# A hybrid layer's projection in another order, with modulation slabs inside it and its blocks gathered by GpSimd

## The chip, the cores and the metric

The kernel runs on one core of one Trainium2 chip, in one launch. The metric is the device time of that launch in microseconds (us), lower is better. Engines are named as the profile names them: PE is TensorE (PEld its weight loads), DVE is VectorE, ACT is ScalarE, POOL is GpSimd, SP is SyncE, which here only issues DMAs.

## The reference

The program is a chain of small layers over 256 tokens of width 1024, all in float32: a hybrid mixer, a conformer convolution, two HGRN mixers, an mLSTM, an S5 mixer, each with a feed-forward layer behind it. Only the first, the hybrid mixer, is touched. Of it:

```python
def ada_terms(cond, w_mod, b_mod):
    m = jax.nn.silu(cond) @ w_mod + b_mod          # "modulation": 6 x 1024 values a layer
    return jnp.split(m, 6, axis=-1)

def split_hybrid_projection(p, conv_w, a_log, dt_bias, q_norm, k_norm):
    qkv = jax.nn.silu(depthwise_conv_centred(p[..., :OFF_Z_A], conv_w))
    ...
    qa = l2_normalize(qkv[:, :, 0]) * (A_HEAD_DIM ** -0.5)
    ka = l2_normalize(qkv[:, :, 1])
    va = qkv[:, :, 2]
    za = p[..., OFF_Z_A:OFF_BA_A]
    beta = jax.nn.sigmoid(ba[:, :, 0])
    g = -jnp.exp(a_log) * jax.nn.softplus(ba[:, :, 1] + dt_bias)
    qb = rms_norm(p[..., OFF_Q_B:OFF_K_B], q_norm)
    kb = rms_norm(p[..., OFF_K_B:OFF_V_B], k_norm)
    vb = p[..., OFF_V_B:]

def gated_delta_chunked(q, k, v, g, beta, s0, need_out):
    ...
    lower = jnp.where(strict, jnp.einsum("nbhcd,nbhsd->nbhcs", kb, kc) * decay, 0.0)
    sol = lax.linalg.triangular_solve(lower + eye, rhs, left_side=True, lower=True, unit_diagonal=True)
```

The mixer projects 256 latent and 256 context tokens, runs a gated delta rule in both directions over four heads ("A"), an attention with eight query heads over two key heads ("B"), and multiplies both results, side by side, by `w_out`. The kernel works the triangular solves out as inverses of 128 x 128 unit lower triangular matrices, 32 of them.

## The kernel before

**Stages.** Each engine has its own program, the stages' parts in order; nothing reorders them. Here the stages are `Front`, `HybridProjection`, `BlockInverse` (which only has work on POOL under its own name), `HybridAttention`, `Delta`, `DeltaReadout`, `BackgroundEnd`, `OutProjection`. Engines meet at semaphores (`wait_ge`, `then_inc`). PE's results go to seven PSUM banks in rotation (`k.job`): a job waits until the bank's user before it is done. An eighth bank belongs to the modulation.

**Weights** come as slabs of 128 x 2048 floats (1 MB) from one DRAM array in the order of use, into a ring of five (`RING`); SP issues the load of a slab once PE is done with the slab five places earlier.

**Projection.** 22 chunks `n` of 128 output features, two to a slab, each eight accumulating matmuls (line 216) over 512 tokens, or 256 where only the latent tokens are wanted. Order: keys A (n 0 to 3, 512 wide), queries A (4 to 7, 256), queries B (8 to 11, 256), keys B and values B (12, 13), values A (14 to 17, 512), the gate z (18 to 21, 256). After n = 8 PE computes the delta rule's gates (line 1331). ACT takes each chunk out of PSUM (lines 1373, 1377); for keys, queries and values A DVE applies a convolution of five taps (lines 1462, 1464), and ACT a silu (1341). The head norms of 13 heads (`heads`): ACT squares (1349), PE sums by a matmul with ones (1305, placed by `sums_after`), ACT takes Ln and Exp (1357, 1360), DVE multiplies (1477). Between the chunks lie also the products of the lower triangles (`lower_after`, lines 1742, 1749, 1729, and on DVE 1808 to 1824) and five rope products (1319), which DVE uses in `rotate` (1488 to 1492).

**Blocks.** The inverses start with their 32 x 32 diagonal blocks, 4 per matrix: `early` (DVE) brings them into one layout by four transposes of 32 partitions each (line 1869), then forward substitution runs in 31 steps of two DVE instructions (`step`, lines 1892 and 1893), ten of them at once and two in each unit of the attention; after units 12 and 13 `scatter_turned` and `scatter` write them back by four transposes each (1899, 1906). `Delta` needs them.

**Attention.** 16 units u. PE: scores (1542), a modulation slab, then for the unit before, four transposes of the probabilities (1550), and every second unit the product with the values (1560), in the others one more modulation slab. ACT: Exp (1577), the copies (470, 1588). DVE: maximum and scaling (1599 to 1604), block steps, copy of the output (1612).

**Background modulation.** `w_mod` has 48 slabs; eight are used in `Front`, 40 lie behind the projection's eleven in the array. `fill(pe, 2)` runs one slab: two small matmuls that turn the row of the slab before (line 398, which wait for ACT's copy at line 470), and eight with the slab (216, `weight_ring,silu_cond`). 25 slabs run in the attention, 8 in `Delta`, and the rest in `BackgroundEnd`, in front of the output projection:

```python
def finish(self, pe):
    self.fill(pe, 2 * len(self.work))
    self.turn(pe, len(self.work) - 1).then_inc(self.done[0], 1)
```

`DeltaReadout` normalizes the delta rule's output in two halves t: ACT copy and square (2259, 2261), PE sum (2252), ACT Ln (2266) and Exp (2269), DVE (2278 to 2283).

## Time and profile before

| | us |
|---|---|
| median of 3 runs | 2736.01 |
| lowest and highest of them | 2727.53, 2738.37 |
| profiled execution | 2733.76 |
| its span in the trace | 2731.9 |

| engine | busy us | share of the span |
|---|---|---|
| PE | 2425.6 | 89% |
| PEld | 2169.8 | 79% |
| DVE | 1556.2 | 57% |
| ACT | 1064.9 | 39% |
| POOL | 90.0 | 3% |

Busy time counts instructions that do work; PE's ends are modelled, so a busy PE isn't PE at its peak. PE has a granted clock, given by the profile as a share of full speed: 1.00 is 2.4 GHz and 0.50 is 1.2 GHz. Of the chain of work that ended last PE holds 79%, DVE 13%, ACT 5%. The hybrid mixer takes the first 460 us or so of the span.

### The profile page before, as it was taken

To read this page: it belongs to the slowest core of one execution; us is meant where nothing else is said; L and a number is where in the kernel's file an instruction comes from. 1 tells how busy PE (TensorE), PEld (TensorE's weight loads), DVE (VectorE), ACT (ScalarE), POOL (GpSimd) and SP (SyncE) were. 2 spreads that over 40 slices of the span, in tenths; PEclk is the share of its full clock that TensorE was granted. 3 is DMA by queue.
4 is the path that set the end of the run, shared out by engine and by line. 5 is a ranking of instruction groups with operands and counts; after the bars stand their busy time and mean duration, and the time that the engine had idled before them with its cause. 6 is when DMAs were issued, how large, how long until landed. Compare 5 with 4: busy or idle time off the path is not lost.

```text
span 2731.9 us, 40134 instructions
## 1 busy us (share of the span) xinstructions
PE 2425.6 (89%) x16978; PEld 2169.8 (79%) x16978; DVE 1556.2 (57%) x2585; ACT 1064.9 (39%) x1675; POOL 90.0 (3%) x107
## 2 busy tenths in 40 slices
PE   7989888999979999768998978998998999748998
PEld 3655666998868998758997858997678998746998
DVE  3475542654846544565657446556955556664655
ACT  2433232434334445333434424434524435623443
POOL 0010000000000000000000000003600000000000
PEclk8998897999999999888999869999999999978999
DMA  7216334553224554203553304552024554301552
GB/s 288 92 63 258 113 125 168 201 186 139 93 77 170 185 185 140 93 1 145 190 190 108 124 17 168 185 184 96 1 77 159 184 185 152 138 1 47 198 189 78
DMA packets 50291, 368.25 MB, mean 135 GB/s; under 512 B 5568, under 2 KB 5696, under 8 KB 5824
## 3 DMA queue, kind: packets, MB, share of 16 engines
q1 hardware_dynamic: 49968, 363.59, 36.6%
q8 instruction: 134, 2.20, 0.3%
q10 hardware_dynamic: 144, 2.10, 0.2%
q14 instruction: 45, 0.37, 0.0%
HBM read 364.62 MB, written 1.05 MB: 134 GB/s over the span
## 4 chain that ended last, share of the span: by engine, by line
PE 79%; DVE 13%; ACT 5%; issue 2%; DMA 1%; SPq 0%; DVEq 0%; ACTq 0%
PE psum L216 63%; PE psum L2755 3%; DVE weight_parts L209 1%; PE psum L3344 1%; PE psum L3345 1%; PE psum L398 1%; PE psum L2378 1%; PE psum L3081 1%; DVE work L947 1%; DMA weight_ring<-stream_dram 1%; PE psum L1560 1%; DVE work L2829 1%; DVE work L2830 1%; PE psum L3362 1%; PE psum L543 1%
## 5 line engine op out<-in xcount | busy, mean ns | idle before, releaser
L216 PE MATMUL psum<-input_parts,weight_parts 128*128 128x256 f32 x7872 | 959.6, 285 | 52.8 <-DVE input_parts L955 27.3
L216 PEld LDWEIGHTS psum<-input_parts,weight_parts 128*128 128x128 f32 x7872 | 954.4, 192 | 60.5 <-issue 54.4
L209 DVE TENSOR_TENSOR weight_parts<-weight_ring,weight_parts 128x1024 fp32r<-128x1024 f32 x484 | 570.5, 1220 | 319.0 <-ACT weight_parts L193 318.4
L193 ACT ACTIVATE weight_parts<-weight_ring 128x1024 fp32r<-128x1024 f32 x484 | 485.3, 1053 | 199.0 <-PE psum L216 193.4
L216 PE MATMUL psum<-work,weight_ring 128*128 128x256 f32 (+1 forms) x1504 | 386.1, 418 | 23.5 <-DVE work L2846 10.2
L216 PEld LDWEIGHTS psum<-work,weight_ring 128*128 128x128 f32 x1504 | 298.0, 199 | 106.7 <-issue 66.5
L216 PE MATMUL psum<-hidden_parts,weight_parts 128*128 128x256 f32 x3168 | 378.9, 281 | 0.0
L216 PEld LDWEIGHTS psum<-hidden_parts,weight_parts 128*128 128x128 f32 x3168 | 376.3, 188 | 0.5
L1036 DVE TENSOR_TENSOR work<-work,psum 128x256 f32<-128x256 f32 x132 | 55.6, 422 | 293.7 <-ACT work L1029 293.7
L1029 ACT ACTIVATE work<-psum 128x256 f32<-128x256 f32 x132 | 50.9, 386 | 426.7 <-PE psum L216 426.6
L2755 PE MATMUL psum<-work 128*128 128x128 f32 x512 | 80.6, 334 | 56.7 <-DVE work L2830 56.7
L2755 PEld LDWEIGHTS psum<-work 128*128 128x128 f32 x512 | 78.3, 247 | 59.2 <-DVE work L2830 59.2
L216 PE MATMUL psum<-weight_parts,input_parts 128*128 128x256 f32 x576 | 74.0, 290 | 12.3 <-DVE weight_parts L209 12.3
L216 PEld LDWEIGHTS psum<-weight_parts,input_parts 128*128 128x128 f32 x576 | 72.6, 196 | 13.6 <-issue 13.6
L216 PE MATMUL psum<-weight_ring,silu_cond 128*32 128x256 f32 x768 | 66.4, 477 | 16.6 <-DMA weight_ring<-stream_dram 16.6
L2780 ACT ACTIVATE work<-work 128x2048 f32<-128x2048 f32 x16 | 30.4, 1910 | 96.9 <-DVE work L2819 96.9
L2421 DVE SCALAR_TENSOR_TENSOR work<-work,vectors 128x256 f32<-128x256 f32 x168 | 67.2, 480 | 0.0
L1040 DVE TENSOR_TENSOR hidden_parts<-work,hidden_parts 128x256 fp32r<-128x256 f32 x132 | 56.2, 426 | 4.5
L398 PEld LDWEIGHTS psum<-constants,modulation_rows 128*128 128x128 f32 x160 | 25.9, 230 | 36.9 <-ACT modulation_rows L470 27.3
L216 PEld LDWEIGHTS psum<-weight_ring,silu_cond 128*32 128x32 f32 x768 | 23.6, 127 | 34.4 <-issue 24.0
L3344 PE MATMUL psum<-work,constants 128*128 128x256 f32 x128 | 39.7, 392 | 12.4 <-DVE work L3422 12.4
L3409 POOL TENSOR_TENSOR work<-constants,columns 128x256 f32<-128x256 f32 x32 | 19.6, 614 | 872.4 <-DVE work L3280 845.7
(460 smaller groups left out, 2349.7 us busy)
## 6 DMA issues: line engine op xcount, KB each, us to landing
weight_ring<-stream_dram SPq DMA_DIRECT2D x341, 1024.0 KB, 4.8
constants<-constants_dram SPq DMA_DIRECT2D x1, 2176.0 KB, 13.8
work<-s_bc_dram ACTq DMA_DIRECT2D x1, 2048.0 KB, 8.4
work<-ctx_dram SPq DMA_DIRECT2D x1, 1024.0 KB, 7.4
residual<-x_dram SPq DMA_DIRECT2D x1, 1024.0 KB, 9.4
out_dram<-residual SPq DMA_DIRECT2D x1, 1024.0 KB, 3.9
vectors<-vectors_dram SPq DMA_DIRECT2D x1, 550.5 KB, 3.5
constants<-constants_dram SPq DMA_DIRECT2D x1, 65.0 KB, 3.5
```

The costliest lines, as they stand in the source:

```text
L193: act.activation(self.parts[:, s % SPLITS, 0, cols], self.ring[:, i % RING, cols], ACT.Identity)\
L209: ins = dve.tensor_tensor(self.parts[:, s % SPLITS, 1, cols], self.ring[:, i % RING, cols], self.parts[:, s % SPLITS, 0, cols].bitcast(F32 ...
L216: mm = pe.matmul(*args, **kw)
L398: return pe.matmul(mod_columns(k, layer, n, 1), rows, k.c("strip_sum"), start=True, stop=True)
L543: mm = pe.matmul(self.job.ap[:, 0:T], self.k.c("mean"), self.sq[:, c, :], start=(c == 0), stop=(c == KC - 1))
L1029: act.activation(self.hid[:, j % 2, :], job.ap[:, 0:T], ACT.Silu).then_inc(self.silu[j][0], 1)
L1036: dve.tensor_tensor(hid, hid, (job if j else self.up_job).ap[:, T:2 * T], ALU.mult).then_inc(self.whole[j][0], 1)
L1040: dve.tensor_tensor(lo, hid, hi.bitcast(F32), ALU.subtract).then_inc(self.ready[j][0], 1)
L2421: ins = dve.scalar_tensor_tensor(acc, src, w, acc, ALU.mult, ALU.add)
L2755: mm = pe.matmul(job.ap[:, i * P:(i + 1) * P], left[:, h, cols], right[:, h, cols], start=True, stop=True)
L2780: act.activation(self.e[:, l % 2, :], self.e[:, l % 2, :], ACT.Exp).then_inc(self.exp[l][0], 1)
L3344: pe.matmul(out, k.c("ident"), t1[:, part, :], start=True, stop=False)
```

## The change

Five edits, all in the hybrid mixer:

- The projection's chunks come in another order: keys A, queries B (n 4 to 7), keys B and values B (8, 9), queries A (10 to 13), values A, z; the weights' columns and all that is placed by n (sums, triangle products, gates, rope) follow.
- After chunks 5, 7, 9, 11, 13, 15 and 17 PE runs one modulation slab (`fill_after`), and ACT takes its row; in the DRAM array these seven slabs stand between the projection's.
- The norms of the four heads of queries A are finished in the attention, one in each of units 1 to 4 (sum on PE, Ln and Exp on ACT, product on DVE); ACT squares them at the projection's end and then loads the table set of Exp and Ln.
- The blocks are gathered and scattered by POOL (`copy`, four copies of 32 partitions each time), and DVE transposes all 128 partitions in one instruction, once in `early` and once each in units 6 and 7.
- 14 block steps run before the attention, and three in each unit from unit 0.

```diff
-EARLY_STEPS = 10
+EARLY_STEPS = 14
+FILL_AFTER = range(5, 18, 2)
...
-        self.chunks = [(kk[:, h, :], every, "conv") for h in range(4)] + [(q[:, h, :], lat, "conv") for h in range(4)]
-        self.chunks += [(qb[:, h, :], lat, "copy") for h in range(4)]
+        self.chunks = [(kk[:, h, :], every, "conv") for h in range(4)] + [(qb[:, h, :], lat, "copy") for h in range(4)]
         self.chunks += [(k.area(H_KB, T2), every, "copy"), (k.area(H_VB, T2), every, "copy")]
+        self.chunks += [(q[:, h, :], lat, "conv") for h in range(4)]
...
-        self.heads = [(self.chunks[n][0], "ones", 1.0) for n in range(8)]
-        self.heads += [(self.chunks[n][0], "ones64", 1.0 / 64) for n in range(8, 13)]
-        self.sums_after = {9: (0, 1), 10: (2, 3), 11: (4, 5), 12: (6, 7), 13: (8, 9), 14: (10, 11), 15: (12,)}
-        self.lower_after = {13: 0, 14: 1, 15: 2, 16: 3}
+        self.heads = [(self.chunks[n][0], "ones", 1.0) for n in range(4)]
+        self.heads += [(self.chunks[n][0], "ones64", 1.0 / 64) for n in range(4, 9)]
+        self.heads += [(self.chunks[n][0], "ones", 1.0) for n in range(10, 14)]
+        self.sums_after = {4: (0, 1), 5: (2,), 6: (3, 4), 7: (5, 6), 8: (7,), 9: (8,)}
+        self.lower_after = {8: 0, 9: 1, 11: 2, 13: 3}
+        self.fill_after = FILL_AFTER
...
+                self.sum_head(pe, i)
+            if n == 6:
                 self.columns.turn(pe)
-            if n == 12:
+            if n == 7:
                 self.columns.sums(pe)
             if n in self.lower_after:
                 self.lower.products(pe, self.lower_after[n])
-            if n == 16:
+            if n in self.fill_after:
+                k.background.fill(pe, 2)
...
             if n >= 18:
-                silu(n - 10)
+                self.silu(act, 2 * n - 32)
+                self.silu(act, 2 * n - 31)
...
+            if n in self.fill_after:
+                k.background.take(act, 2)
+        for i in range(9, 13):
+            self.square(act, i)
+        act.preload_act_table_set(EXP_LN)
...
-        for i in range(8):
+        for i in range(4):
             self.convolve(dve, i)
+        self.normalize(dve, 0)
+        self.normalize(dve, 1)
         self.gate_values(dve)
-        for i in range(8):
+        self.normalize(dve, 2)
+        self.normalize(dve, 3)
+        self.columns.copy(dve)
+        self.columns.finish(dve)
+        for i in range(4, 8):
             self.normalize(dve, i)
-            if i == 5:
-                self.columns.copy(dve)
-        self.columns.finish(dve)
+        self.lower.vector(dve, 0)
         self.normalize(dve, 8)
-        self.normalize(dve, 9)
-        self.lower.vector(dve, 0)
-        self.normalize(dve, 10)
-        self.normalize(dve, 11)
-        self.convolve(dve, 8)
         self.lower.vector(dve, 1)
-        self.normalize(dve, 12)
-        self.convolve(dve, 9)
+        self.convolve(dve, 4)
+        self.convolve(dve, 5)
         self.lower.vector(dve, 2)
-        self.convolve(dve, 10)
-        self.lower.vector(dve, 3)
+        self.convolve(dve, 6)
         dve.wait_ge(k.consts_loaded, 16)
         for i in range(5):
             self.rotate(dve, i)
-        self.convolve(dve, 11)
+        self.convolve(dve, 7)
+        self.lower.vector(dve, 3)
+        for i in range(8, 12):
+            self.convolve(dve, i)
         self.blocks.early(dve)
...
+            if 1 <= u <= 4:
+                k.hyb.sum_jobs.append(k.job(k.hyb.log_ready[8 + u]))
...
+            if 1 <= u <= 4:
+                k.hyb.sum_head(pe, 8 + u)
...
+            if 1 <= u <= 4:
+                k.hyb.root_head(act, 8 + u)
...
+            if 1 <= u <= 4:
+                k.hyb.normalize(dve, 8 + u)
...
-        self.prod = k.spare(W_PROD, BLOCK * BLOCK)
+        self.prod = k.area(H_QD + TT * N4, BLOCK * BLOCK // 4)
         self.a = k.area(H_A32, MATS, P)
         gap = H_B[1] - H_B[0]
         self.b = k.work[:, H_B[0]:H_B[0] + 2 * gap].rearrange("p (s n) -> p s n", s=SEQS)[:, :, 0:MATS // 2 * P]\
             .rearrange("p s (m c) -> p s m c", c=P)
-        self.cleared, self.zero = k.counter("blocks_zero").events(2)
-        self.ready = k.counter("blocks_ready").events(2)
+        self.near = k.spare(W_PROD, BLOCK, BLOCK)
+        self.gathered, *self.ready = k.counter("blocks_zero").events(3)
+        self.turned = k.counter("blocks_turned").events(2)
 
     def gpsimd(self, pool):
         k = self.k
         k.pool.link(pool.memset(self.xc, 0.0))
-        pool.memset(k.spare(W_XC, BLOCK * BLOCK)[:, 0:BLOCK * BLOCK:BLOCK + 1], 1.0).then_inc(self.cleared[0], 1)
-        pool.wait_ge(*k.hyb.turned[4])
+        k.pool.link(pool.memset(k.spare(W_XC, BLOCK * BLOCK)[:, 0:BLOCK * BLOCK:BLOCK + 1], 1.0))
+        pool.wait_ge(*self.lower.l_ready[-1])
+        pool.wait_ge(*self.lower.turned[-1])
+        l = k.spare(W_L, MATS, P)
+        for q in range(BLOCKS):
+            at = self.quarter(q)
+            self.copy(pool, q, self.gathered, self.near[at, :, :], l[at, :, at])
+        k.pool.link(pool.memset(self.a, 0.0))
         pool.wait_ge(*k.hyb.convolved[-1])
-        pool.wait_ge(*self.lower.turned[-1])
-        pool.memset(self.a, 0.0)
+        pool.wait_ge(*k.hyb.normed[-1])
         for s in range(SEQS):
-            ins = pool.memset(self.b[:, s, :, :], 0.0)
-        ins.then_inc(self.zero[0], 1)
+            k.pool.link(pool.memset(self.b[:, s, :, :], 0.0))
+        pool.wait_ge(*self.turned[0])
+        for q in range(BLOCKS):
+            at = self.quarter(q)
+            far = self.lc[at, :, :].rearrange("p r (s m) -> p s m r", s=SEQS)
+            self.copy(pool, q, self.ready[0], self.b[at, :, :, at], far)
+        pool.wait_ge(*self.turned[1])
+        for q in range(BLOCKS):
+            at = self.quarter(q)
+            self.copy(pool, q, self.ready[1], self.a[at, :, at], self.near[at, :, :].rearrange("p s m -> p m s"))
+
+    def copy(self, pool, q, done, out, x):
+
+        ins = pool.tensor_copy(out, x)
+        if q < BLOCKS - 1:
+            self.k.pool.link(ins)
+        else:
+            ins.then_inc(done[0], 1)
+            pool.wait_ge(*done)
+
+    def quarter(self, q):
+        return slice(q * BLOCK, (q + 1) * BLOCK)
 
     def early(self, dve):
 
-        dve.wait_ge(*self.lower.turned[-1])
-        dve.wait_ge(*self.lower.l_ready[-1])
-        l = self.k.spare(W_L, MATS, P)
-        for q in range(BLOCKS):
-            at = slice(q * BLOCK, (q + 1) * BLOCK)
-            ins = dve.transpose(self.lc[at, :, :], l[at, :, at].rearrange("p m s -> p s m"))
-        self.k.dve.link(ins)
-        dve.wait_ge(*self.cleared)
+        dve.wait_ge(*self.gathered)
+        self.k.dve.link(dve.transpose(self.lc, self.near.rearrange("p m s -> p s m")))
         for j in range(EARLY_STEPS):
             self.step(dve, j)
 
     def beside(self, dve, u):
 
-        for j in range(EARLY_STEPS + 2 * u, min(EARLY_STEPS + 2 * u + 2, BLOCK - 1)):
+        for j in range(EARLY_STEPS + 3 * u, min(EARLY_STEPS + 3 * u + 3, BLOCK - 1)):
             self.step(dve, j)
-        if u == 12:
-            dve.wait_ge(*self.zero)
-            self.scatter_turned(dve)
-        if u == 13:
-            self.scatter(dve)
+        if u == 6:
+            dve.transpose(self.lc, self.xc).then_inc(self.turned[0][0], 1)
+        if u == 7:
+            dve.transpose(self.near, self.xc.rearrange("p r s -> p s r")).then_inc(self.turned[1][0], 1)
...
-    def scatter_turned(self, dve):
-
-        for q in range(BLOCKS):
-            at = slice(q * BLOCK, (q + 1) * BLOCK)
-            ins = dve.transpose(self.b[at, :, :, at].rearrange("p s m r -> p r s m"), self.xc[at, :, :])
-        ins.then_inc(self.ready[0][0], 1)
-
-    def scatter(self, dve):
-
-        for q in range(BLOCKS):
-            at = slice(q * BLOCK, (q + 1) * BLOCK)
-            ins = dve.transpose(self.a[at, :, at].rearrange("p m s -> p s m"),
-                                self.xc[at, :, :].rearrange("p r s -> p s r"))
-        ins.then_inc(self.ready[1][0], 1)
...
-    return np.r_[512:1024, 0:512, 2064 + hyb_heads(), 2576:2832, 1024:2048]
+    return np.r_[512:1024, 2064 + hyb_heads(), 2576:2832, 0:512, 1024:2048]
+
+
+def beside_projection(w, mod):
+
+    out, n = [], 0
+    for j in range(len(w)):
+        out.append(w[j:j + 1])
+        if 2 * j + 1 in FILL_AFTER:
+            out.append(mod[n:n + 1])
+            n += 1
+    return np.concatenate(out + [mod[n:]], 0)
```

**PE behind the readout's two sums** (`DeltaReadout`, line 2252 before and 2289 now; line 398 turns a row, `silu_cond` marks a modulation slab, `work,weight_ring` the output projection). Before:

```order
L2252 MATMUL psum<-work,constants 128x512 x2
L398 MATMUL psum<-constants,modulation_rows 128x2 x2
L216 MATMUL psum<-weight_ring,silu_cond 32x256 x8
L398 MATMUL psum<-constants,modulation_rows 128x2 x2
L216 MATMUL psum<-weight_ring,silu_cond 32x256 x8
L398 MATMUL psum<-constants,modulation_rows 128x2 x2
```

and now:

```order
L2112 MATMUL psum<-work 128x128
L2110 MATMUL psum<-spare,work 128x128
L2112 MATMUL psum<-work 128x128
L2289 MATMUL psum<-work,constants 128x512 x2
L398 MATMUL psum<-constants,modulation_rows 128x2 x2
L216 MATMUL psum<-work,weight_ring 128x256 x61
L622 MATMUL psum<-work,constants 128x256
```

The seven slabs between readout and output projection are gone from here; the last row's turn stays.

**ACT in the readout** (Ln is line 2266 before and 2303 now, Exp 2269 and 2306; ACT_TABLE_LOAD brings in a table set). Before:

```order
L2259 ACTIVATE work<-psum 128x512
L2261 ACTIVATE work<-psum 128x512
L2266 ACT_TABLE_LOAD
L2266 ACTIVATE work<-psum,epsilons 128x512
L2269 ACT_TABLE_LOAD
L2269 ACTIVATE work<-work 128x512
```

and now:

```order
L2296 ACTIVATE work<-psum 128x512
L2298 ACTIVATE work<-psum 128x512
L2303 ACTIVATE work<-psum,epsilons 128x512
L2306 ACTIVATE work<-work 128x512
L2296 ACTIVATE work<-psum 128x512
```

The set loaded at the projection's end serves both functions, so the readout has no load left, where it had four in its two halves.

**DVE at the attention's unit 1** now (line 1630 is the maximum, 1944 and 1945 a block step, 1502 the norm's product):

```order
L1630 TENSOR_REDUCE columns<-psum 128x1
L1631 TENSOR_SCALAR columns<-columns 128x1
L1634 RECIPROCAL columns<-columns 128x1
L1635 TENSOR_SCALAR work<-work,columns 128x512
L1944 TENSOR_TENSOR work<-spare 128x252
L1945 TENSOR_TENSOR spare<-spare,work 128x14x18
L1944 TENSOR_TENSOR work<-spare 128x247
L1945 TENSOR_TENSOR spare<-spare,work 128x13x19
L1944 TENSOR_TENSOR work<-spare 128x240
L1945 TENSOR_TENSOR spare<-spare,work 128x12x20
L1502 SCALAR_TENSOR_TENSOR work<-work 128x256
```

Before, the same unit had two steps and no norm.

## Rows read from the trace of the kernel before

**Rows 1.** Windows; busy and count of PE, PEld, DVE, ACT, POOL, then PEclk, DMA, GB/s

```profile
85.30:198.00 112.70, 102.80 (x399) 65.22 (x398) 63.16 (x164) 43.44 (x87) 7.00 (x3) 0.94 0.17 61
198.00:218.00 20.00, 15.13 (x94) 7.10 (x92) 13.44 (x37) 7.27 (x16) 0.00 (x0) 0.70 0.50 174
399.60:432.40 32.80, 22.86 (x147) 12.34 (x148) 3.01 (x6) 11.32 (x17) 0.00 (x0) 0.57 0.57 202
```

**Rows 2.** Timeline of PE in the projection: start, length, instructions, idle before and releaser

```profile
108.16 1.27 PE L1305 MATMUL psum<-work,constants 128*128 128x256 f32 x4 [2.07 <-ACT work L1349]
...
109.95 8.83 PE L216 MATMUL psum<-work,weight_ring 128*128 128x512 f32 x16
...
121.18 7.11 PE L216 MATMUL psum<-work,weight_ring 128*128 128x512 f32 x16
...
172.90 2.07 PE L1319 MATMUL psum<-work,constants 128*128 128x256 f32 x4 [7.35 <-DVE work L1824]
174.77 8.97 PE L216 MATMUL psum<-work,weight_ring 128*128 128x512 f32 x16
```

**Rows 3.** Timeline of ACT and of DVE around the delta rule's gates

```profile
98.51 0.68 ACT L1401 ACTIVATE work<-psum,vectors 8x512 f32<-8x512 f32 x1
...
106.59 0.37 DVE L1447 TENSOR_SCALAR work<-work,columns 8x512 f32<-8x512 f32 x1
```

**Rows 4.** Timeline of PE in attention's first and settled units

```profile
204.71 0.61 PE L398 MATMUL psum<-constants,modulation_rows 128*128 128x2 f32 x4 [3.17 <-ACT modulation_rows L470]
...
233.13 1.12 PE L1542 MATMUL psum<-work 64*128 64x512 f32 x2
234.18 0.61 PE L398 MATMUL psum<-constants,modulation_rows 128*128 128x2 f32 x4
234.72 1.07 PE L216 MATMUL psum<-weight_ring,silu_cond 128*32 128x256 f32 x16
...
243.77 1.12 PE L1542 MATMUL psum<-work 64*128 64x512 f32 x2
```

**Rows 5.** Timeline of DVE, and of ACT, from block transposes to the first Exp

```profile
187.96 7.93 DVE L1869 STREAM_TRANSPOSE spare<-spare 32x1024 f32<-32x1024 f32 x4
...
202.68 0.69 DVE L1599 TENSOR_REDUCE columns<-psum 128x1 f32<-128x512 f32 x1
...
203.60 0.69 ACT L1577 ACTIVATE work<-psum,columns 128x512 f32<-128x512 f32 x1 [2.88 <-DVE columns L1600]
...
209.98 0.42 DVE L1892 TENSOR_TENSOR spare<-spare 128x252 f32<-128x252 f32 x1
```

**Rows 6.** Timeline of DVE in units 12 to 15

```profile
270.93 0.69 DVE L1599 TENSOR_REDUCE columns<-psum 128x1 f32<-128x512 f32 x1 [2.31 <-PE psum L1542]
...
273.26 7.76 DVE L1899 STREAM_TRANSPOSE work<-spare 32x1024 f32<-32x1024 f32 x4
...
283.83 8.82 DVE L1906 STREAM_TRANSPOSE work<-spare 32x1024 f32<-32x1024 f32 x4
292.69 0.69 DVE L1599 TENSOR_REDUCE columns<-psum 128x1 f32<-128x512 f32 x1
...
299.75 0.69 DVE L1599 TENSOR_REDUCE columns<-psum 128x1 f32<-128x512 f32 x1 [0.64 <-PE psum L1542]
```

**Rows 7.** Groups of ACT in 399 to 433; timelines of DVE and PE there

```profile
L2266 ACT ACT_TABLE_LOAD x2 | 2.6, 1283 | 5.7 <-PE psum L2252 5.7
L2269 ACT ACT_TABLE_LOAD x2 | 2.6, 1283 | 0.0
...
411.62 0.69 DVE L2283 TENSOR_TENSOR work<-work 128x512 f32<-128x512 f32 x1
...
431.34 1.01 PE L398 MATMUL psum<-constants,modulation_rows 128*128 128x2 f32 x4 [0.50 <-ACT modulation_rows L470]
```

**Rows 8.** Groups of POOL over the whole span: busy, mean ns of one, idle before

```profile
L3410 POOL TENSOR_SCALAR work<-work 128x256 f32<-128x256 f32 x32 | 34.3, 1071 | 2.8
...
L1852 POOL MEMSET spare<- 128x1024 f32 x1 | 1.0, 952 | 42.5 <-DMA constants<-constants_dram 42.5
```

118 lines of the change are left out of this document (63 added, 55 removed).

## The prediction, made before the changed kernel ran

> **What bounds the kernel now.** The page comes first: PE is busy for 89% of the span and holds 79% of the chain that ended last, so only what shortens PE's program, or its waits, or its slow stretches, counts. Then the windows by stage, in which the reader should look for the gap between a window's length and PE's busy time, and for the granted clock [rows 1]. In the projection (85 to 198 us) PE idles 9.9 us; at the attention's start 4.9 of 20 us, at a mean clock of 0.70; between the readout and the output projection 10 of 32.8 us, at 0.57. Then the timelines of PE and DVE give the waits one by one.
>
> The attention's settled units are PE's own: two units take 10.64 us (233.13 to 243.77), with 0.8 us of idle [rows 4]. The exceptions are its first units and units 12 to 14, where DVE's transposes hold it up [rows 6].
>
> **The end: seven slabs leave.** Before, 40 slabs are spread as 25 in the attention, 8 in `Delta` and 7 behind the readout. Now 7 + 25 + 8 = 40, so none is left behind the readout. PE then starts the output projection when the readout is done. Before it starts at 431.34 + 1.01 = 432.35 us; the readout's last DVE instruction ended at 412.31 [rows 7]. That alone gives 20.0 us. The readout itself gets shorter: its four table loads (2 + 2, 1.283 us each) lie one behind the other on ACT's path to that last instruction, since nothing but the readout's own sums stands between them [rows 7]. They go: 5.1 us. Until now the slabs covered them, so they are worth something only together with the first edit. Together 432.35 - (412.31 - 5.13) = 25.2 us. What is late next is the readout's own chain of PE, ACT and DVE. Both programs enter the output projection after idle PE time, so the clock's recovery is left as it is (0 to 3 us in favour if it doesn't fall this time).
>
> The weights of the output projection are four slabs, in a ring of five that has been filling since `Delta`: no wait.
>
> **The projection: seven slabs enter.** PE has no idle time here to hide them in, so they cost their full time: 0.54 for the turn (234.18 to 234.72) and 1.0 for the slab, 1.54 x 7 - 0.54 (the first has no turn) = 10.2 us [rows 4]. The data is no problem: DMA is busy for 0.17 of this stretch [rows 1]. SP issues the slabs in the array's order, so each of the seven moves a later projection slab back by one load, while PE takes some 14 us for a slab of 512-wide chunks (7.11 per chunk) [rows 2].
>
> What leaves: the waits of 2.07 and 7.35 us, each followed by a stretch of half clock, in which the next chunk takes 8.83 and 8.97 us instead of 7.11: 1.7 and 1.9 us [rows 2]. The four sums of queries A move into the attention: 108.16 shows two of them in 1.27 us, so some 2.0 us for four. A wait of half a us goes as well. Sum 15.5 us. The large wait goes because DVE's `rotate` now comes before `lower.vector(3)` and the five rope jobs find free banks.
>
> What comes: the transpose of the gates (`columns.turn`) now stands after n = 6. ACT takes the gates only behind chunk 5. By PE's program n = 5 ends near 83.6 us, ACT's squares last until 84.8; from ACT's first gate instruction to DVE's last, 98.51 to 106.96, take 8.4 us [rows 3], so the gates are ready near 93.3; PE is done with its sums at 90.2. A new wait of 3.1 us, and as after the 2.07 us wait a slow stretch, 1.8 us. Behind the waiting PE stands chunk 7. Two short waits follow, for `rotate` and for the last triangle, some 1.4 us in all. Sum 10.2 + 3.1 + 1.8 + 1.4 = 16.5 us. The projection ends 1.0 us later, at 198.8 (bounds: -5 if no slow stretch comes and the short waits vanish, +6 if each new wait costs what the 7.35 us one did).
>
> **The attention's start.** Before, DVE spent 7.93 us on the transposes and then 6.8 on ten steps, reached the maximum of unit 0 at 202.68, and ACT's first Exp began at 203.60 [rows 5]. Now DVE gets the last convolution's chunk at about 183.5 (the end less four 256-wide chunks and a slab), ends it at 187.5, transposes once for 2.0 us and makes 14 steps (6.8 + 4 x 0.88, the latter from the pair of instructions around 209.98 [rows 5]): ready at 199.8. A wide transpose isn't in the trace; the nearest rows are 1.98 for 32 partitions (a quarter of 7.93) and 7.93 for all four. I take 2.0, because every other DVE row has the same time per free element whatever it holds, and keep 7.9 as the other end.
>
> The Trainium skill has this in Vector Engine (DVE) Microarchitecture Reference, section 3.8: the transposing front end sustains one element per cycle per lane, in each bank of 32. By that page 128 partitions cost what 32 do, an estimate of 1.1 us for 1024 elements; the trace doesn't agree on the size, 1.98 us, and the sum would be the same by either, since DVE isn't last here.
>
> Late instead is ACT: behind the last z chunk it has two silus, four squares (some 0.35 apart), a table load of 1.28 and a copy of 0.6, 4.6 us in all, so its first Exp starts at 198.8 + 4.6 = 203.4. Gain 0.2 us.
>
> **Units 1 to 4.** Each gets a norm: PE's sum at the unit's end (0.5 us), ACT's Ln and Exp (0.9), DVE's product (0.4), and only then DVE's next maximum and ACT's next Exp. Before, DVE ran ahead of this; now a unit's end is tied to the next one's Exp. Step by step behind the sum, even unit: 0.9 + 0.4 + maximum and scaling 0.9 + Exp 0.9 + row copy 0.4 + probabilities' copy 0.6 + value product 2.0 + sum 0.5 = 6.6, with semaphore time 6.8 us. Odd unit: the same up to the row copy, then turn and slab, sum: 5.7 us. Four units 25.0 against 2 x 10.64 [rows 4]: +3.7 us. The third block step (0.9 us) fits below that: DVE needs 2.3 + 2.7 + 0.9 = 5.9 us at most. The first units keep their waits (3.17 us before the first turn [rows 4]), so I leave the slow stretch after them as long as it was.
>
> **Units 6 to 16.** The eight narrow transposes (7.76 and 8.82 us) go. Units 12 to 14 took 292.69 - 270.93 = 21.76 instead of 10.64 us, and the next 7.06 instead of 5.85 at half clock: 11.1 + 1.2 = 12.3 us [rows 6]. The two wide ones now (2.0 to 2.2 each) stand in units 6 and 7 where block steps were, 1.7 us a unit; DVE then has 4.3 us of work in a unit of 5.3. They cost nothing. If they cost 7.8 and 8.8, all of the 12.3 returns.
>
> **POOL's copies.** 12 copies of 32 partitions x 1024 elements; no POOL copy is in the trace. Bounds: a memset of 1024 elements, 0.95 us, and the dearest row, 1.071 us for 256 elements, times four, 4.3 us [rows 8]. I take 2.5. The gather can start at about 160 us, when the last triangle is turned, and DVE wants it at 187.5: room for 6.8 us a copy. The eight scatter copies lie between unit 6 (near 244) and `Delta` (near 300): 7 us a copy. So nothing at either bound.
>
> The Trainium skill, GPSIMD Engine Reference, section 3.1, speaks against this move: it gives about 2.6 cycles per element on GpSimd against 1 on VectorE. An estimate by that page is 2.2 us a copy; the trace agrees in kind (0.614 us there for 256 two-input elements), and the sum stays as it is, because the work leaves an engine on the path for one that is idle.
>
> **Sum.** -0.2 (start of the attention) + 3.7 - 12.3 - 25.2 = -34.0 us. `Delta` is unchanged, and everything behind the mixer is only shifted. The profiled execution took 2733.76 us with a span of 2731.9, and the median is 2.3 us above it: 2736.0 - 34.0 = 2702.0.
>
> **Rivals.**
> - No slow stretch in the first units. Low clock ruled there from about 206 to 223 us. DVE's earlier start speaks for it, the 3 us of waits that stay against it. Some 7 us more are gained: 2695.
> - The coupling in units 1 to 4 keeps PE at half clock through unit 5. For it: at 411 to 432 us the clock stayed at half with idles of only 0.5 us per slab. Against: at half clock PE has no idle at all in these units. Three more units at some 4.5 us each: 2715.
> - Wide transposes cost as much as four narrow ones: 12.3 returns, and DVE becomes late at the start by 5.9 - 3 us: 2717.
> - The slabs inside the projection cost more than they should (the change moves the work but doesn't save it: new waits for ACT's row copy or for data behind each one, 2 to 3 us each): 7 x 2.5 more, 2720. Against: DMA at 0.17, and ACT is idle for most of the stretch [rows 1].
> - Slower than before: POOL's copies. A copy of C us makes DVE late by 4C - 27 in `early` and `Delta` late by 8C - 56. That eats the 34 us at C = 9.8. At C = 12: 61 us lost, 2763. It takes 2.3 times the dearest row of POOL, and strided rows of 32 elements would have to be the reason.
>
> **How the numbers follow.** Forecast 0.58 (own range 2694 to 2711), no slow stretch 0.13, slow coupling 0.12, dear transposes 0.05, dear slabs 0.06, POOL 0.04, the rest 0.02 for no change by something I don't see. The range for 8 in 10 takes in the first three and the bounds of the projection: 2689 to 2717. A measurement of this kernel tells 0.5% (13.7 us) from no change, so faster means below 2722: the first four and half of the fifth, 0.91; within 0.5%: 0.05; slower: 0.04.
>
> **What the profile after will show.** Right: no `silu_cond` matmuls between the readout's sums and the output projection, no table load in the readout, PE's first output matmul 25 us earlier against `Delta`'s start; one STREAM_TRANSPOSE of 128 partitions near 2 us, POOL copies of 1 to 4 us, no unit near 11 us after unit 6; a wait of about 3 us before the gates' transpose. Wrong, and then the forecast is wrong too: the attention's units 1 to 5 near 10 us each, POOL as releaser of DVE's transpose or of `Delta`'s first matmuls, or waits before each slab in the projection.

## The result, and the profile of the changed kernel

The changed kernel takes 2696.57 us (median of 4 runs, 2694.89 to 2699.72); the kernel before, run beside it, 2731.77 us. The ratio is 0.9871, with a 95% interval from 0.9849 to 0.9893: 35.2 us less. The prediction said 2702, which is 34.0 us below the 2736.0 us that it started from. The profiled span is 2697.9 us, against 2731.9.

The windows by stage: projection, the attention's start, the rest of it up to `Delta`, the readout. Columns as in [rows 1].

```profile
35.50:195.40 159.90, 155.87 (x668) 98.04 (x669) 91.09 (x223) 52.78 (x104) 9.79 (x7) 0.97 0.37 140
195.40:218.00 22.60, 18.09 (x106) 9.31 (x105) 13.26 (x34) 10.04 (x23) 0.00 (x0) 0.70 0.49 180
218.00:296.20 78.20, 70.53 (x569) 40.94 (x567) 34.81 (x80) 27.34 (x67) 19.49 (x10) 1.00 0.72 274
387.50:395.40 7.90, 2.52 (x11) 1.18 (x9) 3.17 (x8) 3.60 (x6) 0.00 (x0) 0.89 0.00 0
```

PE's idle time in the projection fell to 4.0 us (159.90 - 155.87), the attention's start still runs at a mean clock of 0.70, and what was a stretch of 32.8 us at 0.57 [rows 1] is 7.9 us long. PE's timeline in the readout, which answers to the last row of [rows 7]:

```profile
387.51 1.02 PE L2289 MATMUL psum<-work,constants 128*128 128x512 f32 x2
391.09 1.10 PE L2289 MATMUL psum<-work,constants 128*128 128x512 f32 x2 [2.56 <-ACT work L2298]
...
395.35 2.04 PE L216 MATMUL psum<-work,weight_ring 128*128 128x256 f32 x4 [2.82 <-DVE work L2320]
```

No slab and no table load is left; the output projection starts 7.84 us after the first sum, before it was 33.68. PE in the projection, behind chunk 6, then the two short waits (compare [rows 2]):

```profile
89.97 0.99 PE L1670 MATMUL psum<-constants,work 8*128 8x8 f32 x8 [2.91 <-DVE work L1472]
90.89 6.54 PE L216 MATMUL psum<-work,weight_ring 128*128 128x256 f32 x16
...
140.30 1.56 PE L1320 MATMUL psum<-work,constants 128*128 128x256 f32 x6 [0.45 <-DVE work L1857]
...
157.47 0.63 PE L1762 MATMUL psum<-constants,work 128*128 128x128 f32 x4 [0.63 <-DVE work L1857]
```

The wait for the gates came as predicted, 2.91 us, and the next chunk took 6.54 us, where a chunk of this width takes 3.62 (76.64 in the same timeline). PE at the attention's start (compare [rows 4]):

```profile
201.17 0.61 PE L398 MATMUL psum<-constants,modulation_rows 128*128 128x2 f32 x4 [1.50 <-ACT modulation_rows L470]
...
206.25 1.01 PE L398 MATMUL psum<-constants,modulation_rows 128*128 128x2 f32 x4 [2.22 <-ACT modulation_rows L470]
207.19 1.93 PE L216 MATMUL psum<-weight_ring,silu_cond 128*32 128x256 f32 x16
...
252.15 1.96 PE L1587 MATMUL psum<-work 128*128 128x256 f32 x8 [1.97 <-ACT work L1617]
```

A slab takes 1.93 us from 207 us on (1.07 up to 199): half clock, until 216 us (the window from 206 to 216 us has a mean of 0.50, the one from 216 to 218 us 0.98). And DVE, the wide transposes of lines 1924, 1933 and 1935, and the scaling of the probabilities, line 1635, which takes 0.49 us elsewhere:

```profile
184.45 1.97 DVE L1924 STREAM_TRANSPOSE spare<-spare 128x1024 f32<-128x1024 f32 x1
...
234.65 2.14 DVE L1635 TENSOR_SCALAR work<-work,columns 128x512 f32<-128x512 f32 x1
...
239.98 1.24 DVE L1933 STREAM_TRANSPOSE spare<-spare 128x1024 f32<-128x1024 f32 x1
...
245.29 2.28 DVE L1635 TENSOR_SCALAR work<-work,columns 128x512 f32<-128x512 f32 x1
247.50 2.17 DVE L1935 STREAM_TRANSPOSE spare<-spare 128x1024 f32<-128x1024 f32 x1
```

POOL's whole list for this stage: the gather, two clearings, the two scatters.

```profile
158.90 5.36 POOL L1911 COPY spare<-spare 32x1024 f32<-32x1024 f32 x4 [116.70 <-ACT spare L1810]
164.32 3.51 POOL L1894 MEMSET work<- 128x4096 f32 x1
232.84 3.67 POOL L1898 MEMSET work<- 128x2048 f32 x2 [65.01 <-DVE work L1502]
241.35 8.24 POOL L1911 COPY work<-spare 32x1024 f32<-32x1024 f32 x4 [4.84 <-DVE spare L1933]
249.79 8.01 POOL L1911 COPY work<-spare 32x1024 f32<-32x1024 f32 x4 [0.20 <-DVE spare L1935]
```

**Stage times.** I worked these out from PE's and ACT's timelines of each profiled execution, and most of what follows rests on them. Projection: from its first matmul to the attention's first. To Exp: from there to the first Exp. Attention: on to the end of the last value product. `Delta`: on to the readout's first sum. Readout: on to the output projection's first matmul. Median: of the timed runs (one run for the two clearing kernels).

| kernel | projection | to Exp | attention | Delta | readout | sum | median |
|---|---|---|---|---|---|---|---|
| before | 159.04 | 5.77 | 105.22 | 89.72 | 33.68 | 393.43 | 2731.8 |
| after | 159.88 | 4.65 | 96.12 | 91.32 | 7.84 | 359.81 | 2696.6 |
| slabs_at_end | 152.51 | 4.65 | 92.62 | 89.70 | 26.11 | 365.59 | 2713.6 |
| narrow_transposes | 159.92 | 4.65 | 104.38 | 89.70 | 7.85 | 366.50 | 2701.1 |
| before_one_load | 158.05 | 5.75 | 107.95 | 89.71 | 26.32 | 387.78 | 2720.4 |
| loads_in_readout | 159.92 | 4.65 | 94.90 | 89.71 | 13.93 | 363.11 | 2698.1 |
| no_query_norms | 159.94 | 4.65 | 94.49 | 89.69 | 7.85 | 356.62 | 2692.9 |
| long_memsets | 159.76 | 4.65 | 99.12 | 91.31 | 8.79 | 363.63 | 2699.6 |
| short_memsets | 159.24 | 4.65 | 94.82 | 91.30 | 7.85 | 357.86 | 2704.1 |
| both_waits | 158.35 | 3.69 | 88.56 | 89.70 | 7.84 | 348.14 | 2686.5 |
| no_steps_in_unit_0 | 159.74 | 4.64 | 91.30 | 89.71 | 7.84 | 353.23 | 2690.2 |
| all_edits | 150.81 | 3.83 | 87.74 | 89.71 | 8.13 | 340.22 | 2678.1 |

The work ahead of the projection and behind the readout is the same in all of them. Yet in the profiled executions the first lasts 35.5 to 40.4 us and the second 2292 to 2307 us, with the granted clock of the conformer, HGRN, mLSTM and S5 stages falling at other places. So a difference of under 10 us between two medians says little here, and the stage where the edit is says more. The columns differ a little without an edit too: `Delta`, whose code is the same in all runs, is 91.3 us in three traces and 89.7 in the others.

### The profile page after: what moved, and what is told of

It reads as the page before. It is cut to its first block, busy times and chain, and to the rows that moved or that the text cites. A ratio compares the mean times of both kernels' runs of the same rounds, so it can differ in the third digit from the quotient of the medians.

```text
span 2697.9 us, 40129 instructions
## 1 busy us (share of the span) xinstructions
PE 2413.5 (89%) x16978; PEld 2167.0 (80%) x16978; DVE 1545.0 (57%) x2576; ACT 1058.3 (39%) x1671; POOL 111.2 (4%) x119
## 4 chain that ended last, share of the span: by engine, by line
PE 80%; DVE 12%; ACT 5%; issue 2%; DMA 1%; SPq 0%; DVEq 0%; ACTq 0%
PE psum L216 63%; PE psum L2792 3%; DVE weight_parts L209 1%; PE psum L3381 1%; PE psum L3382 1%; PE psum L2415 1%; PE psum L3118 1%; DMA weight_ring<-stream_dram 1%; PE psum L543 1%; DVE work L947 1%; PE psum L398 1%; DVE work L2866 1%; DVE work L2867 1%; PE psum L1587 1%; PE psum L3399 1%
## 5 line engine op out<-in xcount | busy, mean ns | idle before, releaser
L216 PE MATMUL psum<-work,weight_ring 128*128 128x256 f32 (+1 forms) x1504 | 387.2, 419 | 26.5 <-DVE work L2883 10.2
L216 PE MATMUL psum<-weight_ring,silu_cond 128*32 128x256 f32 x768 | 58.2, 426 | 15.7 <-DMA weight_ring<-stream_dram 15.7
```

What stands on the lines that cost most here:

```text
L216: mm = pe.matmul(*args, **kw)
```

## The experiments

### Where the slabs are worth what they cost

```diff
-FILL_AFTER = range(5, 18, 2)
+FILL_AFTER = ()
```

> The changed kernel with no slab inside the projection: all seven stand behind the readout again, everything else as changed. My accounting: the projection gets shorter by 10.2 us (seven slabs of 1.54 us, the first without its turn), and behind the readout each slab costs what it did in the kernel before, 3.38 us at half clock, 23.7 us in all, of which about 1 us lies beside the readout's last steps; so about +12 us against the changed kernel, a ratio to the kernel before near 0.9915. If the clock stays at full there, a slab takes some 2.4 us and the sum is +6 us. Rival: slabs are as dear inside the projection as at the end, because the gain came from the other edits: then within 2 us of the changed kernel, ratio 0.987.

Measured: 2713.6 us, ratio 0.9929 (0.9916 to 0.9943). That is 17.0 us above the changed kernel's median, where +12 was expected. By stages the readout is 18.3 us longer and the projection 7.4 us shorter, +10.9 us; the attention is 3.5 us and `Delta` 1.6 us shorter as well, so the stages say +5.8 us and the rest of the 17.0 lies in work that didn't change. The accounting holds in kind and the rival falls. Both sides are smaller than expected: a slab at the end costs 2.6 us, not 3.38, and the projection gives 7.4, not 10.2 us. PE in its projection shows why the latter:

```profile
95.39 0.67 PE L1670 MATMUL psum<-constants,work 8*128 8x8 f32 x8 [4.11 <-DVE work L1472]
...
141.10 1.56 PE L1320 MATMUL psum<-work,constants 128*128 128x256 f32 x6 [1.99 <-DVE work L1857]
...
157.99 0.63 PE L1762 MATMUL psum<-constants,work 128*128 128x128 f32 x4 [1.88 <-DVE work L1857]
```

The same three waits are 4.0 us longer in sum (7.98 against 3.99 us). So the slabs do hide something: where they stand, the other engines have time to catch up. The first units of the attention also run faster here (gap from the third score matmul to the fourth 6.75 us, 9.02 in the changed kernel); why the clock came back earlier, no run isolates.

### The four table loads

Two runs. In the kernel before, a load of the common table set ahead of the attention makes the readout's four unnecessary; in the changed one, four are put back:

```diff
+        act.preload_act_table_set(EXP_LN)
         act.wait_ge(*self.vt_job.full)
```

> The kernel before with one edit: the table set that serves both logarithm and exponential is loaded ahead of the attention, so that the readout has no load. My accounting: the seven slabs behind the readout cover the four loads of 5.1 us, so the time stays (within 1 us of the kernel before, ratio 1.000). Rival: the loads lie on the path in the kernel before as well and 5.1 us go, ratio 0.998. In the profile: the two sums of the readout get closer by 2.6 us or more, while the output projection starts as long after Delta as before.

```diff
             act.wait_ge(*self.jobs[t].full)
+            act.preload_act_table_set("silu_and_others")
+            act.preload_act_table_set(EXP_LN)
```

> The changed kernel with two table loads added in each half of the readout, behind the wait for the sum, as many as the kernel before had there. My accounting: nothing covers them now, 4 times 1.28 us, so +5.1 us, ratio 0.989. Rival: they are hidden, 0 us, ratio 0.987. A third way: the longer idle of PE in the readout lowers the clock in the output projection, then +8 us or more.

Measured: 2720.4 us, ratio 0.9969 (0.9950 to 0.9987), and 2698.1 us, ratio 0.9875 (0.9857 to 0.9893). The second agrees with the accounting in its stage: the readout is 6.1 us longer. Of that 4.8 us are waits (5.13 and 5.09 us where the changed kernel has 2.56 and 2.82), the rest half clock. The third way falls: the output projection's first 20 us have a mean clock of 0.87 in both. The median moved by 1.5 us only, which is within what the unchanged stages vary. The first is a miss. The readout got 7.4 us shorter, not 0. (The attention got 2.7 us longer there, and I don't know why; the median fell by 11 us, the five stages by 5.65 us.) PE's timeline there:

```profile
401.02 1.02 PE L2253 MATMUL psum<-work,constants 128*128 128x512 f32 x2
404.60 1.10 PE L2253 MATMUL psum<-work,constants 128*128 128x512 f32 x2 [2.56 <-ACT work L2262]
...
405.97 1.07 PE L216 MATMUL psum<-weight_ring,silu_cond 128*32 128x256 f32 x16
407.75 0.61 PE L398 MATMUL psum<-constants,modulation_rows 128*128 128x2 f32 x4 [0.71 <-ACT modulation_rows L470]
...
410.49 1.93 PE L216 MATMUL psum<-weight_ring,silu_cond 128*32 128x256 f32 x16
```

And in the kernel before, not yet shown:

```profile
398.54 1.02 PE L2252 MATMUL psum<-work,constants 128*128 128x512 f32 x2
404.69 2.04 PE L2252 MATMUL psum<-work,constants 128*128 128x512 f32 x2 [5.12 <-ACT work L2261]
...
411.06 1.01 PE L398 MATMUL psum<-constants,modulation_rows 128*128 128x2 f32 x4 [1.83 <-ACT modulation_rows L470]
```

The seven slabs stand behind the second sum in PE's queue, and that sum waits for ACT's squares, which stand behind the first half's loads. So the first two loads (2.56 us) were never covered: PE waited 5.12 instead of 2.56 us. The longer wait also brought half clock at once (2.04 us for the sum); without it the slabs begin at full clock and fall to half with the third. The second half's loads were covered in part: in the kernel before, PE waits 1.83 us for ACT's copy of the first slab's row, which stands behind them, and 0.71 us without them. So of the 7.4 us some 3.7 are waits and the other half is clock.

### The block inverse as before

```diff
-EARLY_STEPS = 14
+EARLY_STEPS = 10
...
-        if u == 6:
-            dve.transpose(self.lc, self.xc).then_inc(self.turned[0][0], 1)
...
+        if u == 12:
+            dve.wait_ge(*self.zero)
+            self.scatter_turned(dve)
...
```

> The changed kernel with the block inverse as before: twelve narrow transposes of 32 partitions on DVE, ten early steps and two a unit, no copies on POOL. The prediction's terms: units 12 to 14 are held up again, +12.3 us, and DVE is late at the attention's start by 5.9 us against a slack of 2.8, +3.1 us: together +15 us, ratio 0.9927. Rival: only units 12 to 14 return and the start is covered by ACT and PE: +12 us, ratio 0.9915. Rival: POOL's new work costs DVE as much as it saves, so that less than +9 us appears.

Measured: 2701.1 us, ratio 0.9892 (0.9871 to 0.9914); the attention takes 8.3 us more, the way to the first Exp the same 4.65 us. DVE's timeline at the two scatters:

```profile
268.91 7.78 DVE L1933 STREAM_TRANSPOSE work<-spare 32x1024 f32<-32x1024 f32 x4
...
279.51 8.81 DVE L1940 STREAM_TRANSPOSE work<-spare 32x1024 f32<-32x1024 f32 x4
```

The gaps between PE's score matmuls at these two are 10.66 and 12.12 us against 4.72 and 5.92: +12.1 us, the predicted 12.3. The +3.1 us at the start was an error in my working (with ten early steps instead of fourteen DVE has 3.5 us less to do, so ACT is last either way). What takes 3.6 us off again is in units 0 to 2: the gaps of the scores there are 10.66 and 6.40 us, 11.67 and 9.02 in the changed kernel. Unit 8 takes 5.92 instead of 7.12 us, 1.2 us off, and small differences elsewhere add 1.0: 8.3 us in all. That is less than the 9 us of the last rival, which is right in part: unit 8 is where POOL's copies stand in the changed kernel (see below). The 3.6 us pointed at the third block step.

### The third block step in unit 0

```diff
-        for j in range(EARLY_STEPS + 3 * u, min(EARLY_STEPS + 3 * u + 3, BLOCK - 1)):
+        for j in range(EARLY_STEPS + 3 * (u - 1), min(EARLY_STEPS + 3 * u, BLOCK - 1)) if u else ():
```

> The changed kernel, only DVE makes no block step in the attention's unit 0 (each unit's three steps and both wide transposes come one unit later). In the changed kernel PE waits 1.50 and 2.22 us in units 0 and 1, the clock falls, and the scores of units 1 to 3 start 11.67 and 9.02 us after one another; with narrow transposes and two steps a unit it was 10.66 and 6.40, with squares and row copy moved as well and no steps in unit 0 6.16 and 6.40. Theory: the third step in unit 0 is what holds the clock down, so the two gaps fall to some 8 and 6.4 us, -6 us. Rival: it is the row copy's place behind the first Exp; then the steps alone give less than 2 us.

Measured: 2690.2 us, ratio 0.9852 (0.9814 to 0.9890). The gaps are 9.62 and 6.60 us, the attention takes 4.8 us less: somewhat under the 6 us of the theory and well over the 2 us of the rival. The edit takes all three steps out of unit 0, not the third alone. In the changed kernel DVE, between the first scaling and the next maximum, makes three steps:

```profile
201.07 0.49 DVE L1635 TENSOR_SCALAR work<-work,columns 128x512 f32<-128x512 f32 x1
201.47 0.42 DVE L1944 TENSOR_TENSOR work<-spare 128x255 f32<-128x255 f32 x1
...
204.22 0.69 DVE L1630 TENSOR_REDUCE columns<-psum 128x1 f32<-128x512 f32 x1
```

2.75 us, and ACT's second Exp, PE's next turn (the 2.22 us wait above) and the clock follow from them. With the steps moved the 2.22 us wait is gone and only the 1.50 us one is left. The clock still falls behind that one (a slab at 206.78 takes 1.93 us) and is back at 211 us. So the steps account for about half of the slow stretch; the rest goes only when the squares and the row copy move too, in both_waits below.

### The norms in units 1 to 4

> The changed kernel without the norms of queries A in the attention's units 1 to 4 (the four sums on PE, their logarithm and exponential on ACT, their product on DVE are left out, so these queries aren't normalized; POOL's second clearing waits for a unit of the attention instead of the last norm). The prediction had +3.7 us for the coupling of the engines. The changed kernel's trace shows PE idle for only 0.3 us where the odd units wait: theory now, nothing but PE's own four sums of 0.5 us and about 0.7 us of waits, so -2.7 us. Rival: the norms also keep the clock down in the first units; then the slow stretch from 206 to 218 us goes and -5 us or more.

Measured: 2692.9 us, ratio 0.9873 (0.9846 to 0.9901); the attention takes 1.6 us less, where 2.7 were expected. In units 3 to 5 the gaps are 4.75, 5.92 and 4.72 us, with the norms 5.59, 6.39 and 5.08, so three norms cost 1.67 us, nearly PE's own sums of 0.5 us. Units 1 and 2 stayed slow without the norms too (10.50 and 10.39 us). The rival falls, and so does the prediction's coupling of 3.7 us.

### DVE beside POOL

Six more clearings by POOL, whole or in pieces of 256 elements:

```diff
+        for _ in range(6):
+            k.pool.link(pool.memset(self.a, 0.0))
```

> The changed kernel with six more clearings of the same 4096 elements by POOL behind its second clearing, 3.5 us each, beside the attention's units 6 to 11. Theory: a TENSOR_SCALAR of DVE from SBUF to SBUF (the scaling of the probabilities, 0.49 us) that begins beside a POOL instruction is held until that instruction ends, so it takes 0.5 to 4 us in each of some five units, 2 us on average; one that lasts over 1.3 us delays PE. Rival: both share bandwidth, then each of them takes about twice 0.49 us and PE isn't late. Second rival: the long ones in the changed kernel had another cause (a wait for a semaphore), then they stay at 0.49 us.

```diff
+        for _ in range(6):
+            for m in range(0, MATS, 2):
+                k.pool.link(pool.memset(self.a[:, m:m + 2, :], 0.0))
```

> As the kernel with six more clearings, but each cut into 16 instructions of 256 elements, so that POOL clears as much in pieces of some 0.3 us. If DVE is held until the POOL instruction at work ends, the scaling now takes at most 0.8 us and PE isn't late. If bandwidth is shared, it takes as long as beside the long clearings.

POOL as a whole, then in order of time two of its clearings, DVE's scalings beside them and the PE product behind, with the long ones:

```profile
238.24 22.00 POOL L1900 MEMSET work<- 128x4096 f32 x6
...
245.71 3.51 POOL L1900 MEMSET work<- 128x4096 f32 x1
...
246.97 2.53 DVE L1635 TENSOR_SCALAR work<-work,columns 128x512 f32<-128x512 f32 x1
...
253.01 3.51 POOL L1900 MEMSET work<- 128x4096 f32 x1
...
253.20 3.60 DVE L1635 TENSOR_SCALAR work<-work,columns 128x512 f32<-128x512 f32 x1
...
253.87 2.38 PE L1587 MATMUL psum<-work 128*128 128x256 f32 x8 [2.03 <-ACT work L1617]
```

With the short ones:

```profile
239.99 36.60 POOL L1901 MEMSET work<- 128x256 f32 x96
...
259.34 0.67 DVE L1635 TENSOR_SCALAR work<-work,columns 128x512 f32<-128x512 f32 x1
...
265.00 1.97 PE L1587 MATMUL psum<-work 128*128 128x256 f32 x8 [0.78 <-ACT work L1617]
```

The two clearings end at 249.22 and 256.52 us. The scalings end at 249.50 and 256.80, 0.28 us behind each. So DVE's instruction is held until POOL's ends. It isn't bandwidth that is shared: beside 256-element pieces POOL is at work without a break too, and the scaling takes 0.53 to 0.69 us for the whole 36.6 us, ending 0.27 or 0.28 us behind the end of a piece. The gaps between the scores are 7.59 and 7.25 us beside the long ones, 4.72 and 5.92 everywhere beside the short ones. In POOL's busy time the pieces cost 36.6 instead of 22.0 us. The Trainium skill has the rule in SBUF — State Buffer, section SBUF: two separate sides: the port pair that DVE and GpSimd share is an exclusive lock for the whole instruction, and not a split of bandwidth. These two traces agree.

### Both waits taken away

```diff
+            if n == 7:
+                self.columns.turn(pe)
             for i in self.sums_after.get(n, ()):
                 self.sum_head(pe, i)
-            if n == 6:
-                self.columns.turn(pe)
...
-        for i in range(9, 13):
-            self.square(act, i)
         act.preload_act_table_set(EXP_LN)
...
+        k.background.take(act, 2)
         for u in range(len(self.units) + 1):
...
-            k.background.take(act, 2)
+            if u:
+                k.background.take(act, 2)
+            else:
+                for i in range(9, 13):
+                    k.hyb.square(act, i)
```

with no block steps in unit 0, as above.

> The changed kernel with two edits. One: the transposes of the delta rule's gates stand behind chunk 7, ahead of the sums there, not behind chunk 6, where PE waits 2.91 us and the next chunk takes 6.54 instead of 3.62 us. Two: the attention starts otherwise; the four squares of queries A stand behind the first Exp, the first slab's row is copied by ACT ahead of it, and DVE makes no block step in unit 0 (its steps and both wide transposes come one unit later); there PE waits 1.50 and 2.22 us before the first turns, and the clock is at half from 206 to 218 us. Theory: -5.8 us in the projection; -4 us in the attention if the slow stretch stays as long, -9 us if it goes; together -10 to -15 us against the changed kernel, a ratio to the kernel before near 0.982. Rivals: the gates' values only meet PE one chunk later, and the waits of the first units move to the transposes of the probabilities; then less than 3 us are gained.

Measured: 2686.5 us, ratio 0.9852 (0.9827 to 0.9878), and 11.7 us less in the stages, of which 1.6 are `Delta`'s. The attention's side is as hoped: the first Exp 1.0 us earlier, gaps of 6.16 and 6.40 us, no half clock (the window from 194.2 to 218 us has a mean of 1.00 where it was 0.70), 7.6 us less. The projection gave 1.5 us, not 5.8:

```profile
93.61 2.83 PE L1687 MATMUL psum<-columns,constants 128*128 128x4 f32 x16 [0.96 <-DVE columns L1701]
...
99.09 8.17 PE L216 MATMUL psum<-work,weight_ring 128*128 128x512 f32 x16
```

The 2.91 us wait is gone, but 0.96 us came up before the sums over the gates, and the clock still went down: a mean of 0.75 from 93.6 to 107.1 us. A wait of a third of the length cost the same slow stretch (in the changed kernel the window from 90.0 to 103.5 us has 0.75 as well).

### The version that beats both

```diff
-FILL_AFTER = range(5, 18, 2)
+FILL_AFTER = range(5, 14, 2)
...
             if n == 7:
+                k.background.fill(pe, 2)
                 self.columns.sums(pe)
...
-            k.pool.link(pool.memset(self.b[:, s, :, :], 0.0))
+            for m in range(0, MATS // 2, 2):
+                k.pool.link(pool.memset(self.b[:, s, m:m + 2, :], 0.0))
```

with no second slab behind chunk 7, and with `k.background.fill(pe, 2)` behind each of the readout's two sums, its row copy on ACT behind the second square.

> The kernel with both waits taken away, and three edits more. One: the slab behind chunk 7 stands between the gates' transposes and the sums over them, where PE waited 0.96 us and the clock fell to half for 13 us. Two: of the seven slabs five stay in the projection and one each goes behind the two sums of the readout, where PE waits 2.56 and 2.82 us. Three: POOL's second clearing is cut into pieces of 256 elements. Expected by the traces: -4.3 us in the projection for the wait and the slow stretch, -3.1 us for two slabs, up to +0.5 us in the readout, -0.8 us in unit 6; together -7 us against the kernel with both waits taken away, 18 to 19 us below the changed kernel by the traces up to the output projection, a ratio to the kernel before near 0.981. Rival: ACT's row copies and the last turn don't fit in the readout's gaps and cost what the slabs saved there, then -5 us.

Measured: 2678.1 us (2672.8 to 2682.2), ratio 0.9805 (0.9781 to 0.9830), 18.5 us below the changed kernel's median; by stages 7.9 us below the kernel with both waits taken away. PE, at the gates and in the readout:

```profile
95.82 1.07 PE L216 MATMUL psum<-weight_ring,silu_cond 128*32 128x256 f32 x16
96.82 1.95 PE L1688 MATMUL psum<-columns,constants 128*128 128x4 f32 x16
98.63 7.11 PE L216 MATMUL psum<-work,weight_ring 128*128 128x512 f32 x16
...
372.18 1.07 PE L216 MATMUL psum<-weight_ring,silu_cond 128*32 128x256 f32 x16
374.75 1.10 PE L2296 MATMUL psum<-work,constants 128*128 128x512 f32 x2 [1.50 <-ACT work L2306]
```

The slab now covers the 0.96 us, and the next chunk takes 7.11 us, full clock. Projection -7.5 us (of it 3.1 for two slabs), readout +0.3 us for those two slabs. The gap of scores beside POOL's second clearing, 6.75 us with both waits taken away, is 5.92. One gain the five stages don't count: the output projection's first 20 us now run at a clock of 1.00, in the changed kernel at 0.87. The edits were only run together; that each did its part is read from its stage.

## Why the prediction was right, and where its steps were not

The terms, from the stage times and the scores' starts:

| term | predicted | measured |
|---|---|---|
| projection | +1.0 | +0.84 |
| its end to the first Exp | -1.2 | -1.12 |
| first Exp to unit 6 | +3.7 | +1.97 |
| unit 6 to the attention's end | -12.3 | -11.07 |
| `Delta` | 0 | +1.60 |
| readout | -25.2 | -25.84 |
| sum | -34.0 | -33.62 |

Ahead of the projection the profiled execution was 3.25 us shorter, and behind the readout 2.87 us longer, both by work that didn't change; the spans differ by 34.0 us. That the sum came within 0.4 us is partly luck: the attention's two parts missed by 1.7 and 1.2 us in opposite directions, and 1.6 us came up in `Delta`, where nothing was predicted.

- **The end** was right as a sum. Its split into 20.0 for slabs and 5.1 for loads covered by them was not: slabs_at_end and before_one_load give 18.3 and 7.4 us. The step "until now the slabs covered them" failed; I looked at what is busy beside the loads and not at what waits for them in PE's queue. The clock was worth about half of the 7.4 us, and my term for the loads had no clock in it.
- **The projection's** sum holds, by terms that leaned on each other. The slow stretch behind the gates' wait was 2.9, not 1.8 us; the short waits 1.08, not 1.4; the seven slabs took PE 9.7 us (seven times 1.0, and six turns of 0.45), not 10.2. "PE has no idle time here to hide them in" failed: the old order had 9.9 us of idle time [rows 1], and in the new one without slabs PE waits 8.0 us, with them 4.0. So leaving the slabs out gains only 7.4 us.
- **The attention's start**: ACT was last, as said, DVE waited 2.81 us for the first Exp's output. DVE's wide transpose took 1.97 us for an assumed 2.0.
- **Units 1 to 4** is the mis-sized term: 3.7 predicted, 1.97 measured, and 1.6 by no_query_norms. The chain that I added up step by step isn't on the path: PE waits 0.17 and 0.29 us in the odd units. The norms cost their matmuls, 0.5 us each.
- **"The third block step fits below that"** failed: in unit 0 it doesn't, and no_steps_in_unit_0, which moves all three steps, gets 4.8 us back. My rival of a vanished slow stretch, 7 us, was the state of both_waits (7.6 us); the steps in unit 0 kept it away, together with the squares and the row copy at the attention's start.
- **Units 12 to 14**: 12.3 predicted, 12.1 us by narrow_transposes. 1.2 us were given back in unit 8, which takes 7.12 instead of 5.92 us: the value product at 252.15 waits 1.97 instead of 0.78 us. Before it DVE's scaling at 245.29 took 2.28 instead of 0.49 us beside POOL's scatter, and the wide transpose of 2.17 us followed. With both one unit later (both_waits) the scalings beside the scatter take 1.13 to 1.76 us and no unit there is longer than 5.92 us, so what the two cost depends on the unit that they fall in. My step "so nothing at either bound" only asked whether POOL is in time, not what DVE may do meanwhile.
- **POOL's copies** took 1.34 us (gather) and 2.06 us (scatter) each for an assumed 2.5. The estimate of 2.2 us in the prediction took 2.6 cycles per element from the Trainium skill, GPSIMD Engine Reference, section 3.1; the section explains that figure by the two inputs of a tensor_tensor, and a copy has one.
- **`Delta`** lost 1.6 us between 351 and 360 us, where PE's unchanged work ran at half clock from 352.6 to 356.0 us. It did so in three of the twelve traces (after, long_memsets, short_memsets), though the code there is the same in all; the cause is open.

## What to carry to other kernels

Before calling a delay covered by filler work, ask whether the filler stands ahead of the delayed instruction or behind it in the in-order queue: behind it, it covers nothing of that wait. Put filler work where a wait is rather than where there is room, because the slow clock that a wait can bring may be dearer than the wait (13.5 us at a mean of 0.75 behind a wait of 0.96 us, which the slab placed there took away). Not every wait brings it: the 0.78 us before each value product left the settled units at 1.00. And when work moves to an idle GpSimd, look at what it does to DVE: each long instruction holds up a scaling from SBUF to SBUF until its end. Clearings cut into pieces did so for 0.2 us at most, at the price of more POOL time (36.6 instead of 22.0 us); the copies were not cut in any run.

## What the runs showed of the hardware

- A DVE TENSOR_SCALAR from SBUF to SBUF of 0.49 us lasts until the POOL instruction beside it ends and 0.28 us more, up to 3.60 us beside a clearing of 4096 elements (long_memsets). Four SCALAR_TENSOR_TENSOR of line 1489, beside POOL's gather, took 5.11 us instead of 3.11 in the changed kernel.
- A wide transpose costs the same 1.97 us as a narrow one of as many elements per partition ([rows 5]: 7.93 us for four). Where its source isn't strided (line 1933) it took 1.24 us.
- A POOL copy of 32 partitions x 1024 elements took 1.34 us in the gather and 2.06 us in the scatter.
- The same unchanged work, some 2300 us long, varied by 15 us between executions of kernels that differ only ahead of it.
